# Routing of tokens in pieces inside the output stage of a mixer-and-experts layer, with a shorter hand-over to the experts

## Chip, cores, metric

One core of a Trainium2 chip runs the whole layer as one program. The metric is the device time of one execution in microseconds (us). TensorE (PE), VectorE (DVE), ScalarE (ACT), GpSimd (POOL) and the DMA issuer SyncE (SP) each run their own instruction stream and meet at semaphores.

## The reference, cut to what matters

2048 prompt tokens and 64 sample tokens (8 sequences of 8) go through one layer. The mixers leave `[y_pool, y_lru]`; after them come

```
mix = concat([y_pool, y_lru]) @ w_out
x1  = LN(ALPHA * x + (1 + g1) * mix) * ln1_g + ln1_b
u2  = x1 * (1 + sc2) + sh2
group logits = u2 @ w_group + b_group (4), expert logits = u2 @ w_route + b_route (4 x 4)
group = argmax; the top 2 experts inside it; weights = softmax(top 2) * softmax(group)[group]
y   = sum over the token's 2 experts of weight * (silu(u2 @ w_gate) * (u2 @ w_up)) @ w_down
out = LN(ALPHA * x1 + (1 + g2) * y) * ln2_g + ln2_b
```

All of it is fp32 (D = 1024, 16 experts of width 256).

## The kernel before

The 2112 tokens are 17 tiles of 128 (`NT`; the last has 64 rows). The program has four stages: the conditioning, input projection and mixers (to about 497 us in the trace); the **output stage** (to 735 us); the **routing** (to 791 us); the **experts** and the last layer norm (to the end). Each engine's instructions are in an order written out by hand, and each wait is a semaphore written by hand. fp32 products on PE are made of three matmuls of split operands (hi and lo parts), lines L1583 to L1585.

**Output stage, tile t.** PE: `out_proj` makes 48 matmuls of 512 columns in two halves of 24; inside the second half, after 9 of them (`k == 3`), stand the eight transposes of tile t-2 (`turn_u2`, L1534), and behind it the router of tile t-2 (`router`, L1736, 20 columns, waits for the evacuated transposes and for `rt_ok`). DVE: `ln_in(t)` (L1202 from PSUM, L1206, statistics L1212 to L1220), `ln_out(t-1)` (L1228, L1229: u2 of the tile, on which `turn_u2` waits), `router_out(t-2)` (L1233, signals `rt_ok`). ACT splits operands, takes the root, normalises (L831) and evacuates transposes. POOL makes, in turns, the lo part of a left operand (`y_lo(t+2)`, L587) and x1 of a tile in two whole-tile instructions (`x1_tile(t)`, L602 and L603); `ln_out(t)` waits for these two. SP stores x1 and u2 of each tile and loads the next operands.

**Routing**, all on DVE and for all 17 tiles at once: choices of group and experts (L1276 to L1296, each step waits for the one before), `m_ready`; PE counts, for 272 columns (tile, expert), the tokens ahead within a tile and in the tile (L1768, L1769); a running sum over the 17 tiles (L1307, 17 steps), the slots of each expert (L1310 to L1315), each token's row (L1318 to L1331), then three large one-hot tables (`hot_b`, L1340 to L1342; `hot_a`, L1345) from which 34 bf16 matmuls (L1774) make the token list `tok_i` (L1364). A **slot** is 128 rows of one expert; there are 48. POOL gathers the tokens of a slot with an indirect DMA (L637). Meanwhile expert 0's weights (SP, L446, issued after `rt_ok` 17) are split by ACT (L875) and POOL (`first_lo`, L623, six parts). Then DVE makes the routing weights (L1367 to L1378) and three weight tables (L1381, L1383), and PE another 34 matmuls (L1826) ahead of the first expert matmul. Each slot is then `gate_up`, `turn_x` of the next slot, `turn_h` and `down` on PE, with evacuations (L893, L1422) on ACT and DVE.

```
            with pe.Fori(2, NT // 2) as j:
                for b in range(2):
                    out_proj(2 * j + b, b, turn_before=lambda: turn_u2(2 * j + b - 2, b))
                    router(2 * j + b - 2)
```

Of the kernel before, what the change touches and what calls it, by code (L numbers as in the profile page):

```python
# [5 lines left out]
P = 128  # L6
D = 1024
KD = D // P
SEQ, DEC_B, DEC_T = 2048, 8, 8
# [20 lines left out]
OUT_EARLY = 6  # L30
ARENA = 21168
# [5 lines left out]
NZ = 6  # L37
# [47 lines left out]
def build(nc, A):  # L85
    with ExitStack() as ctx:
# [37 lines left out]
        def part_at(off, *shape):  # L124
# [53 lines left out]
        w_raw = [at(n * WE, WE) for n in (1, 0)]  # L178
# [10 lines left out]
        ln2_g, ln2_b, g2_s = at(6144, D), at(7168, D), at(8192, D)  # L189
        zt = [at(n * 1024, D) for n in (*range(6), *range(9, 20))]  # L190
        y_pair = [place(ada_arena, n * 1024, D) for n in range(2)]

        rt = [at(n * 272, NT, NE) for n in range(6)]
        rt_f = [at(1632 + n * 68, NT, NGR) for n in range(9)]
        r17 = [at(2248 + n * NT, NT) for n in range(10)]
        big_t = at(2424, NE, NT)
        lt_prod = at(2700, NE, NE)
        slot_ge = at(2960, SLOTS, NE)

        hot_b = at(14336, 3 * NT * SLOTS).bitcast(BF16).rearrange("p (k t v s) -> p k t v s", k=2, t=NT, v=3)  # L200
        hot_a = at(16784, 2 * NT * P // 2).bitcast(BF16).rearrange("p (k t r) -> p k t r", k=2, t=NT)
        tile_no = at(4146, 2, NT)
        e48 = [at(4184 + n * SLOTS, SLOTS) for n in range(10)]
        e16 = [at(3960 + n * NE, NE) for n in range(5)]
# [38 lines left out]
        pos_i = sb("pos_i", [P, 2, NT], I32)  # L243
# [21 lines left out]
            u2T_ok rt_mm rt_ok m_ready cnt_mm w_exp w_expd hot_ready idx_mm idx_ready w_raw0 w_raw1 xg0 xg1 xgT_mm  # L265
# [3 lines left out]
        z_in = [sem(f"z_in{n}") for n in range(NZ)]  # L269
        pair_in = sem("pair_in")  # L270

        ada_in = [sem(f"ada_k{k}") for k in range(KD)]
# [25 lines left out]
        def raw_part(buf, n):  # L298

            return w_raw2[:, ds(buf * -1 + 1, 1), n * SPLIT:(n + 1) * SPLIT].rearrange("p a n -> p (a n)")  # L300
# [7 lines left out]
        def _(sp):  # L308

            sp.dma_start(z_d[NTOK:NTOK + P, :], xpt_d[0]).then_inc(S["dump_in"], 16)  # L310
            for k in range(KD):
                sp.dma_start(w_ada[k], ada_d[k][:, 0:2048]).then_inc(ada_in[k], 16)
# [192 lines left out]
            for t in range(NT - 1):  # L505
# [3 lines left out]
                if t >= NZ:  # L509
                    sp.wait_ge(z_in[t % NZ], 16 * (t // NZ))  # L510
# [1367 lines left out]
```

## Time and profile before

| | |
|---|---|
| three runs | 1355.7, 1356.63 (median), 1358.93 us |
| the profiled execution | 1357.65 us; its span in the trace 1355.8 us |
| mean granted TensorE clock | 0.915 |
| busy in the span | PE 1129.9 us (83%), DVE 912.4 (67%), ACT 538.3 (40%), POOL 528.5 (39%) |
| output stage, routing, experts, last norm | to 735, to 792, to 1263, to 1356 us |

The shares are means over stages with different limits. The routing is a stretch of 56 us in which PE stands nearly still and DVE is the busy engine; in the output stage and with the experts it is the reverse. How PE's clock is read: 1.00 is its higher level (2.4 GHz), 0.50 its lower one (1.2 GHz), values between are means over a stretch that holds both.

### The profile page before, as it was taken

What the parts mean: (1) busy time and instruction counts of PE and PEld (TensorE: products, weight loads), DVE (VectorE), ACT (ScalarE), POOL (GpSimd) and SP (SyncE); (2) the same over time, 40 slices, a digit from 0 to 9 for tenths busy, and PEclk for the clock granted to TensorE, in tenths of its full rate; (3) what the DMA queues carried; (4) which work ended last, traced back from release to release, by engine and by line L of the source; (5) the groups of instructions that cost most, each with busy time, mean ns of one, the idle gap of its engine ahead of it and who ended that gap; (6) DMA issues with size and microseconds to landing.
All of it is one profiled execution on the core that took longest, in us unless ns stands there. A gap on an engine that the chain in (4) does not pass through costs nothing.

```text
span 1355.8 us, 23133 instructions
## 1 busy us (share of the span) xinstructions
PE 1129.9 (83%) x6461; PEld 940.3 (69%) x6462; DVE 912.4 (67%) x1844; ACT 538.3 (40%) x917; POOL 528.5 (39%) x540
## 2 busy tenths in 40 slices
PE   4889999999998688999995169999999999999200
PEld 1278988898888567888884057777777777888200
DVE  2675988898889485555554966556676666534398
ACT  0345435543542631222221134446555554433232
POOL 1411202220220225656652434545655464543365
PEclk8779999999998788999996589999999999999755
DMA  9604113312321463443435077887988887654673
GB/s 339 249 1 163 56 67 124 124 39 85 124 77 55 131 218 123 152 144 139 170 116 170 17 253 209 231 226 220 251 257 246 223 223 210 132 116 92 171 287 116
DMA packets 106187, 215.04 MB, mean 159 GB/s; under 512 B 18091, under 2 KB 67759, under 8 KB 103187
## 3 DMA queue, kind: packets, MB, share of 16 engines
q1 hardware_dynamic: 85004, 163.14, 34.8%
q0 software_dynamic: 20736, 50.89, 16.8%
q10 hardware_dynamic: 415, 0.63, 0.1%
q8 instruction: 15, 0.25, 0.1%
q14 instruction: 17, 0.14, 0.0%
HBM read 153.93 MB, written 85.96 MB: 177 GB/s over the span
## 4 chain that ended last, share of the span: by engine, by line
PE 57%; DVE 20%; DMA 6%; issue 6%; ACT 4%; DVEq 2%; SPq 2%; POOL 1%; ACTq 1%; POOLq 0%
PE bank L1583 16%; PE bank L1585 15%; PE bank L1584 15%; PE bank L1534 5%; DMA ada_arena<-in_w_ada 2%; PE bank L1658 2%; DVE arena L1515 1%; PE bank L1604 1%; DVE st L1498 1%; DVE arena L1206 1%; DVE parts L1415 1%; PE bank L1736 1%; DMA arena<-in_w_up 1%; DVEq L1408 1%; ACT parts L888 1%
## 5 line engine op out<-in xcount | busy, mean ns | idle before, releaser
L1583 PE MATMUL bank<-parts 128*128 128x256 f32 (+2 forms) x1616 | 570.7, 353 | 38.7 <-DVE parts L1422 15.9
L1585 PE MATMUL bank<-parts 128*128 128x256 f32 (+2 forms) x1616 | 554.2, 343 | 0.0
L1584 PE MATMUL bank<-parts 128*128 128x256 f32 (+2 forms) x1616 | 553.7, 343 | 0.0
L1583 PEld LDWEIGHTS bank<-parts 128*128 128x128 f32 x1616 | 310.1, 192 | 86.8 <-issue 36.2
L1585 PEld LDWEIGHTS bank<-parts 128*128 128x128 f32 x1616 | 309.5, 192 | 35.1
L1584 PEld LDWEIGHTS bank<-parts 128*128 128x128 f32 x1616 | 310.4, 192 | 31.5
L570 POOL TENSOR_TENSOR arena<-arena 128x256 f32<-128x256 f32 (+1 forms) x36 | 25.9, 722 | 311.9 <-DVE h_last L1139 276.6
L1534 PE MATMUL bank<-ident,arena 128*128 128x128 f32 (+3 forms) x792 | 120.4, 285 | 32.5 <-DVE arena L1229 12.9
L1534 PEld LDWEIGHTS bank<-ident,arena 128*128 128x128 f32 (+3 forms) x792 | 95.8, 148 | 64.3 <-issue 20.5
L1415 DVE TENSOR_TENSOR parts<-arena,parts x90 | 104.8, 1220 | 18.9 <-ACT parts L888 18.9
L913 ACT ACTIVATE arena<-bank,w_now 128x512 f32<-128x512 f32 x96 | 66.1, 688 | 126.4 <-PE bank L1585 72.9
L1449 DVE SCALAR_TENSOR_TENSOR arena<-bank,w_now,arena 128x512 f32<-128x512 f32 x96 | 69.3, 749 | 48.2 <-PE bank L1585 48.2
L888 ACT ACTIVATE parts<-arena x90 | 88.7, 1056 | 5.9 <-DMA arena<-in_w_down 5.9
L650 POOL DMA_INDIRECT z_d<-arena,dst_now x48 | 80.8, 1684 | 19.0 <-issue 19.0
L729 ACT ACTIVATE arena<-bank,proj_b 128x256 f32<-128x256 f32 x64 | 30.4, 475 | 142.2 <-PE bank L1585 142.2
L602 POOL TENSOR_TENSOR arena<-arena 128x1024 f32<-128x1024 f32 (+1 forms) x17 | 56.6, 3327 | 55.7 <-ACT arena L831 55.7
L1202 DVE TENSOR_TENSOR arena<-bank,arena 128x512 f32<-128x512 f32 (+1 forms) x34 | 21.8, 683 | 83.3 <-PE bank L1585 83.3
L893 ACT ACTIVATE parts<-bank 128x512 fp32r<-128x512 f32 x96 | 52.2, 595 | 37.0 <-PE bank L1534 34.6
L1422 DVE TENSOR_TENSOR parts<-bank,parts 128x512 fp32r<-128x512 f32 x96 | 61.8, 685 | 7.5 <-ACT parts L893 7.5
L898 ACT ACTIVATE arena<-bank 128x256 f32<-128x256 f32 x48 | 18.4, 384 | 108.9 <-PE bank L1585 107.7
L644 POOL COPY dst_now<-dst_i 128x2 int32 (+1 forms) x48 | 8.7, 181 | 130.6 <-ACT arena L913 130.6
L652 POOL DMA_INDIRECT ysamp_d<-arena,dst_now x48 | 53.6, 1116 | 14.6 <-issue 14.6
(270 smaller groups left out, 1538.5 us busy)
## 6 DMA issues: line engine op xcount, KB each, us to landing
arena<-in_w_gate SPq DMA_DIRECT2D x16, 1024.0 KB, 5.6
arena<-in_w_up SPq DMA_DIRECT2D x16, 1024.0 KB, 9.7
arena<-in_w_down SPq DMA_DIRECT2D x16, 1024.0 KB, 13.0
arena<-in_w_ada SPq DMA_DIRECT2D x14, 1024.0 KB, 5.7
ada_arena<-in_w_ada SPq DMA_DIRECT2D x8, 1024.0 KB, 17.0
arena<-in_x_prompt SPq DMA_DIRECT2D x8, 1024.0 KB, 6.9
yT_d<-arena SPq DMA_DIRECT2D x16, 512.0 KB, 5.1
arena<-yT_d SPq DMA_DIRECT2D x16, 512.0 KB, 4.7
```

Source lines behind the costliest of these rows:

```text
L602: o.step(pool.tensor_tensor(x1[b][0:n, :], z[b][0:n, :], row_tiles[0:n, 1, :], ALU.mult))
L650: pool.indirect_dma_start(out=z_d, out_offset=bass.IndirectOffsetOnAxis(ap=dst_now[b][:, 0:1], axis=0), in_=y_sb[b], in_offset=None, compu ...
L652: pool.indirect_dma_start(out=ysamp_d, out_offset=bass.IndirectOffsetOnAxis(ap=dst_now[b][:, 1:2], axis=0), in_=y_raw[b], in_offset=None, ...
L888: act.activation(part(w_hi, e & 1, n), raw_part(e & 1, n), ACT.Copy).then_inc(S["w_hi"], 1)
L913: act.activation(y_raw[b][:, 512 * h:512 * h + 512], bank[5 + h][:, :], ACT.Copy, scale=w_now[b][:, 0:1]).then_inc(S["y_act"], 1)
L1415: dve.tensor_tensor(part(w_lo, e & 1, n), raw_part(e & 1, n), part(w_hi, e & 1, n).bitcast(F32), ALU.subtract).then_inc(S["w_lo"], 1)
L1422: dve.tensor_tensor(xT_lo[:, k, :], bank[h][:, :].rearrange("p (k n) -> p k n", n=P), xT_hi[:, k, :].bitcast(F32), ALU.subtract).then_inc( ...
L1449: dve.scalar_tensor_tensor(y_sb[b][:, cols], bank[5 + h][:, :], w_now[b][:, 0:1], g2_row[:, cols], ALU.mult, ALU.mult).then_inc(S["y_dve"], 1)
L1534: return pe.transpose(out, in_, ident[0:rows, 0:rows])
L1583: pe.matmul(out, x_hi, w_hi, start=start, stop=False)
L1584: pe.matmul(out, x_hi, w_lo, start=False, stop=False)
L1585: return pe.matmul(out, x_lo, w_hi, start=False, stop=stop)
```

## The change

- **Routing by groups of tiles.** `ROUTE = ((0, 4), (4, 8), (8, 12), (12, 17))`. For a group (lo, hi), DVE makes the choice of group behind `ln_out` of step t = hi + 2 (7 instructions), the choice of experts behind that of step hi + 3 (19), and the rows with their part of `hot_a` behind that of step hi + 5 (9). PE makes a group's ranks (two matmuls of 64 columns) in step hi + 5. So steps 6, 7, 9, 10, 11, 13, 14 and 15 carry a piece; the rows of tiles 8 to 11 and all of tiles 12 to 16 are done behind the stage. The running sum over tiles is part of the choices, and the 17-step sum and the 272-column count are gone.
- **PE of the stage.** `router(t-3)` stands between the two halves of `out_proj(t)` instead of `router(t-2)` behind it; the transposes stand after 18 matmuls of the second half (`k == 6`) instead of 9. DVE's `router_out` is ahead of `ln_in`.
- **The stage's end.** DVE makes `ln_out(15)` ahead of `ln_in(16)`, and makes x1 of the last tile itself (2 instructions, L1347 and L1348 of the new file) in place of POOL.
- **Weights of experts 0 and 1.** Expert 0's load waits for the last x1, expert 1's for the last router output (before: for the weights of all slots). `first_lo`: parts 0 and 1 on POOL ahead of the gathers, 4 and 5 behind the first two gathers, parts 2 and 3 on DVE. ACT makes the scaled one-hot piece (`hot_part`) that DVE made.
- **Token list.** The one-hots are made in two halves with PE starting on the first; `tok_i` is ahead of the list of the slots' experts; a first `idx_ready` releases the gathers, a second everyone else.
- **Routing weights.** The three tables and 34 matmuls stand behind `gate_up(0)`, `turn_x(1)` and `turn_h(0)`.
- Buffers are placed anew; the last stage's loads have 8 semaphores instead of 6.

The diff, cut (`-` before, `+` after):

```
-            router_out(1)
-            with dve.Fori(2, NT // 2) as j:
-                    ln_in(2 * j + b, b, P, prompt_rows, j + 1)
-                    ln_out(2 * j + b - 1, 1 - b, P, prompt_rows, j + b, False)
-                    router_out(2 * j + b - 2)
+            for t in range(3, NT - 1):
+                router_out(t - 3)
+                ln_in(t, t % 2, P, prompt_rows, t // 2 + 1)
+                ln_out(t - 1, 1 - t % 2, P, prompt_rows, (t - 1) // 2 + 1, False)
+                for lo, hi in ROUTE:
+                    if t == hi + 2: choose_group(lo, hi)
+                    if t == hi + 3: choose_experts(lo, hi)
+                    if t == hi + 5: place_rows(lo, hi)
...
-                        if turn_before is not None and h == 1 and k == 3:
+                        if turn_before is not None and h == 1 and k == 6:
...
+            def ranks(lo, hi):
+                pe.wait_ge(S["m_ready"], i + 1)
+                pe.matmul(out[:, 0:n * NE], tri[:], flat(m_all[:, lo:hi]), start=True, stop=False)
+                pe.matmul(out[:, 0:n * NE], ones[:], flat(cum_all[:, lo:hi]), start=False, stop=True).then_inc(S["rank_mm"], 1)
+            def route(t):
+                router(t - 3, first=t == 3)
+                for lo, hi in ROUTE:
+                    if t == hi + 5: ranks(lo, hi)
+            for t in range(3, NT - 1):
+                out_proj(t, t % 2, turn_before=lambda: turn_u2(t - 2, t % 2), between=lambda: route(t))
...
             turn_x(0, 0, 1, first=True)
+            gate_up(0, 0)
+            turn_x(1, 1, 1)
+            turn_h(0)
             pe.wait_ge(S["hotw_ready"], 1)
...
-            gate_up(0, 0)
-            turn_x(1, 1, 1)
-            turn_h(0)
```

What it does to the order of instructions, at three places. First DVE in the output stage, behind `ln_in` of a middle tile. Before (L1228, L1229 are `ln_out`; L1233 `router_out`; then the loop begins again):

```order
L1228 TENSOR_TENSOR arena<-arena 128x1024 [waits u2T_mm]
L68 REGISTER_ALU
L1229 TENSOR_TENSOR arena<-arena 128x1024 [waits dve_order]
L1233 ISA [waits rt_mm]
L1233 TENSOR_TENSOR logits<-bank,arena 128x20
L1252 REGISTER_ALU
L1252 COMPARE_AND_BRANCH
```

In the change, step 7 (L1246 is the end of `ln_out`; L1263 to L1297 `choose_experts` of tiles 0 to 3; L1250 `router_out` and L1219 the next tile's `ln_in`):

```order
L1246 TENSOR_TENSOR arena<-arena 128x1024 [waits dve_order]
L1263 TENSOR_REDUCE ada_arena<-ada_arena 128x4
L1264 TENSOR_TENSOR ada_arena<-ada_arena 128x16 [waits dve_order]
L1265 TENSOR_TENSOR ada_arena<-ada_arena,prio 128x16 [waits dve_order]
...
L1292 TENSOR_TENSOR ada_arena<-ada_arena 128x64
L1294 TENSOR_TENSOR ada_arena<-ada_arena 128x64 [waits dve_order]
L1296 TENSOR_TENSOR ada_arena<-ada_arena 128x16 [waits dve_order] x4
L1297 MEMSET spare 1x1 [waits dve_order]
L1250 TENSOR_TENSOR logits<-bank,arena 128x20 [waits rt_mm]
L1219 TENSOR_TENSOR arena<-bank,arena 128x512 [waits mix_ready]
```

Nineteen instructions and a signal, nearly all of them waiting for DVE's own last result (`dve_order`), now stand between one tile's `ln_out` and the next tile's `router_out` and `ln_in`, where before the loop went straight on.

Second, DVE at the end of the stage, from the last tile's statistics on. Before (the two pairs L1228 and L1229 are `ln_out` of tiles 15 and 16; L1276 the first choice):

```order
L1228 TENSOR_TENSOR arena<-arena 128x1024 [waits u2T_mm,u2_st1,x1_ready]
L1229 TENSOR_TENSOR arena<-arena 128x1024 [waits dve_order]
L1233 TENSOR_TENSOR logits<-bank,arena 128x20 [waits rt_mm]
L1228 TENSOR_TENSOR arena<-arena 64x1024 [waits u2T_mm,u2_st0,x1_ready]
L1229 TENSOR_TENSOR arena<-arena 64x1024 [waits dve_order]
L1233 TENSOR_TENSOR logits<-bank,arena 128x20 [waits rt_mm]
L1233 TENSOR_TENSOR logits<-bank,arena 64x20 [waits rt_mm]
L1276 TENSOR_REDUCE arena<-logits 128x17 [waits consts,rt_ok]
```

In the change (L1245 and L1246 are `ln_out`, L1219 begins `ln_in(16)`, L1250 is a router output, L1305 begins the rows of tiles 8 to 11):

```order
L1245 TENSOR_TENSOR arena<-arena 128x1024
L1246 TENSOR_TENSOR arena<-arena 128x1024
L1219 TENSOR_TENSOR arena<-bank,arena 64x512 x2
...
L1250 TENSOR_TENSOR logits<-bank,arena 128x20
L1347 TENSOR_TENSOR arena<-arena 64x1024
L1348 TENSOR_TENSOR arena<-arena 64x1024
L1245 TENSOR_TENSOR arena<-arena 64x1024
L1246 TENSOR_TENSOR arena<-arena 64x1024
L1250 TENSOR_TENSOR logits<-bank,arena 128x20
L1305 TENSOR_TENSOR ada_arena<-ada_arena,bank 128x2x64
...
L1250 TENSOR_TENSOR logits<-bank,arena 64x20
L1263 TENSOR_REDUCE ada_arena<-logits 128x5
```

`ln_out(15)` (the first L1245, L1246) has moved ahead of the last tile's `ln_in` (L1219), the last x1 (L1347, L1348) has come in from POOL, and the rows of tiles 8 to 11 (from L1305) stand ahead of the last router output and the last choices (from L1263).

Third, PE behind the last router. Before (L1768 and L1769 are the counts, L1774 the token list's matmuls, L1534 the transposes of slot 0, L1826 the weight matmuls):

```order
L1768 MATMUL bank<-arena,tri 128x272 [waits m_ready]
L1769 MATMUL bank<-arena,ones 128x272
L1774 MATMUL bank<-arena 128x144 [waits hot_ready]
L1774 MATMUL bank<-arena 128x144 x16
...
L1534 MATMUL bank<-ident,arena 128x128 [waits xg0,idx_ready]
L1534 MATMUL bank<-ident,arena 128x128 x7
L1826 MATMUL bank<-arena 128x144 [waits hotw_ready]
L1826 MATMUL bank<-arena 128x144 x33
```

In the change (L1831 to L1833 are the counts and ranks of the last group, L1858 the token list, L1602 the transposes, L1651 the first expert matmul's wait):

```order
L1831 MATMUL bank<-ada_arena,ones 128x16 [waits m_ready]
L1832 MATMUL bank<-ada_arena,tri 128x80
L1833 MATMUL bank<-ada_arena,ones 128x80
L1858 MATMUL bank<-arena,ada_arena 128x144 [waits hot_part,hot_ready]
L1858 MATMUL bank<-arena,ada_arena 128x144 x16
...
L1602 MATMUL bank<-ident,arena 128x128 [waits xg0,idx_ready]
L1602 MATMUL bank<-ident,arena 128x128 x7
...
L1651 REGISTER_ALU [waits w_lo]
...
L1651 MATMUL bank<-parts 128x512
```

The 272-column counts have shrunk to 16 and 80 columns, and the 34 weight matmuls are gone from between the transposes and the first expert matmuls; they stand behind the 24 matmuls of `gate_up(0)` and ten transposes.

## Rows read from the trace of the kernel before

**Rows 1.** By stretch: length, busy PE, PEld, DVE, ACT, POOL; PEclk, DMA, GB/s.
```profile
717.44:735.60 18.16, 10.17 (x63) 9.25 (x62) 9.58 (x17) 4.69 (x7) 5.64 (x2) 0.65 0.28 87
735.60:742.70 7.10, 0.00 (x0) 0.00 (x0) 6.34 (x24) 0.00 (x0) 0.00 (x0) 0.50 0.84 270
742.70:767.50 24.80, 2.18 (x4) 1.17 (x4) 21.41 (x44) 6.16 (x8) 14.17 (x6) 0.50 0.18 71
767.50:780.50 13.00, 3.77 (x34) 3.30 (x34) 12.61 (x18) 0.00 (x0) 0.00 (x0) 0.62 0.00 1
780.50:791.70 11.20, 5.21 (x41) 4.84 (x42) 10.26 (x26) 2.48 (x3) 6.17 (x9) 0.54 0.40 121
791.70:813.20 21.50, 16.86 (x84) 13.32 (x81) 9.91 (x20) 9.36 (x14) 5.28 (x6) 1.00 0.95 330
```

**Rows 2.** PE timeline, first transposes of the stage and matmuls after (start, duration, idle before).
```profile
516.05 1.97 PE L1534 MATMUL bank<-ident,arena 128*128 128x128 f32 x8 [3.54 <-DVE arena L1229]
...
519.10 0.63 PE L1583 MATMUL bank<-parts 128*128 128x512 f32 x1
519.52 0.63 PE L1584 MATMUL bank<-parts 128*128 128x512 f32 x1
...
522.45 0.39 PE L1584 MATMUL bank<-parts 128*128 128x512 f32 x1
522.68 0.40 PE L1585 MATMUL bank<-parts 128*128 128x512 f32 x1
```

**Rows 3.** Waits of PE in 515 to 720 us (total, times, longest).
```profile
PE bank L1534 <- DVE arena L1229: 6.3, 6, 3.5
```

**Rows 4.** PE timeline, a router inside the stage.
```profile
689.91 1.86 PE L1736 MATMUL bank<-arena 128*128 128x20 f32 x16
```

**Rows 5.** DVE timeline, one tile of the stage.
```profile
634.24 1.29 DVE L1202 TENSOR_TENSOR arena<-bank,arena 128x512 f32<-128x512 f32 x2 [6.04 <-PE bank L1585]
635.67 3.33 DVE L1206 SCALAR_TENSOR_TENSOR arena<-arena 128x1024 f32<-128x1024 f32 x1
...
642.72 1.22 DVE L1229 TENSOR_TENSOR arena<-arena 128x1024 f32<-128x1024 f32 x1
```

**Rows 6.** POOL timeline, the two x1 instructions of that tile.
```profile
642.83 3.35 POOL L602 TENSOR_TENSOR arena<-arena 128x1024 f32<-128x1024 f32 x1 [4.91 <-ACT arena L831]
646.26 2.40 POOL L603 TENSOR_TENSOR arena<-arena 128x1024 f32<-128x1024 f32 x1
```

**Rows 7.** DVE timeline, end of the stage: `ln_out` of tiles 15 and 16.
```profile
722.26 1.23 DVE L1228 TENSOR_TENSOR arena<-arena 128x1024 f32<-128x1024 f32 x1
...
729.41 1.22 DVE L1228 TENSOR_TENSOR arena<-arena 64x1024 f32<-64x1024 f32 x1 [4.58 <-POOL arena L603]
```

**Rows 8.** DVE timeline, routing: small steps, slots, one-hot tables.
```profile
751.18 1.77 DVE L1312 TENSOR_SCALAR arena<-arena 128x16 f32<-128x16 f32 x1
752.98 9.46 DVE L1313 TENSOR_TENSOR arena<-lt,arena 128x256 f32<-128x256 f32 x1
...
762.93 0.17 DVE L1315 TENSOR_TENSOR arena<-arena 128x16 f32<-128x16 f32 x1
763.14 0.17 DVE L1317 TENSOR_SCALAR arena<-arena 128x16 f32<-128x16 f32 x1
...
767.49 1.86 DVE L1340 TENSOR_TENSOR arena<-iota_s,pos_f 128x1632 bf16<-128x1632 f32 x1
...
769.94 1.85 DVE L1342 TENSOR_TENSOR arena<-arena 128x1632 bf16<-128x1632 bf16 x1
771.83 4.76 DVE L1345 TENSOR_TENSOR arena<-iota_r,pos_f 128x2176 bf16<-128x2176 f32 x2
```

**Rows 9.** POOL timeline, the lo parts of expert 0.
```profile
747.98 14.17 POOL L623 TENSOR_TENSOR parts<-arena,parts 128x1024 fp32r<-128x1024 f32 x6 [18.60 <-ACT parts L875]
```

**Rows 10.** PE timeline, token list and routing weights.
```profile
774.31 3.89 PE L1774 MATMUL bank<-arena 128*128 128x144 bf16 x34 [29.42 <-DVE arena L1345]
...
788.43 3.51 PE L1826 MATMUL bank<-arena 128*128 128x144 bf16 x34 [0.62 <-DVE arena L1383]
```

More of the change, by code:

```diff
@@ L30 @@
 OUT_EARLY = 6
+ROUTE = ((0, 4), (4, 8), (8, 12), (12, 17))
+FIRST_DVE = (2, 4)
+FIRST_HI = 3
 ARENA = 21168
@@ L624, in _ @@
                                    ALU.subtract).then_inc(S["w0_lo"], 1)
+            for n in range(FIRST_DVE[0]):
+                first_lo(n)
             pool.wait_ge(S["idx_ready"], 1)
@@ L656, in _ @@
             gather(1, 1)
+            for n in range(FIRST_DVE[1], E_PARTS):
+                first_lo(n)
             for n in range(2, 6):
@@ new lines, in choose_experts @@
+            def choose_experts(lo, hi):
+                n = hi - lo
+                hot_g, hot_1, hot_2, esel = (f[:, 0:n] for f in f_b[0:4])
+                over_e = hot_g.unsqueeze(3).to_broadcast([P, n, NGR, EPG])
+                first_max(esel, n, m1[:, lo:hi], hot_1)
+                o.step(dve.scalar_tensor_tensor(esel, hot_1, -BIG, esel, ALU.mult, ALU.add))
+                first_max(esel, n, m2[:, lo:hi], hot_2)
+                if hi == NT:
+                    o.step(dve.tensor_tensor(hot_g, hot_g, bc(valid[:, lo:hi], NGR), ALU.mult))
+                for k, hot in enumerate((hot_1, hot_2)):
+                    o.did(dve.tensor_tensor(g4(e12[:, k, lo:hi]), over_e, hot.unsqueeze(2).to_broadcast([P, n, NGR, EPG]), ALU.mult))
+                o.wait()
+                o.step(dve.tensor_tensor(m_all[:, lo:hi], e12[:, 0, lo:hi], e12[:, 1, lo:hi], ALU.add))
+                for t in range(lo, hi):
+                    o.step(dve.tensor_tensor(cum_all[:, t + 1], cum_all[:, t], m_all[:, t], ALU.add))
+                dve.memset(spare[0:1, 0:1], 0.0).then_inc(S["m_ready"], 1)
@@ L1247, in _ @@
             dve.wait_ge(S["rt_in"], 64)
-            router_out(0)
-            ln_in(3, 1, P, prompt_rows, 2)
-            ln_out(2, 0, P, prompt_rows, 2, False)
-            router_out(1)
-            with dve.Fori(2, NT // 2) as j:
-                o.enter(j, 2, LN_STEPS)
-                for b in range(2):
-                    ln_in(2 * j + b, b, P, prompt_rows, j + 1)
-                    ln_out(2 * j + b - 1, 1 - b, P, prompt_rows, j + b, False)
-                    router_out(2 * j + b - 2)
@@ L1258, in _ @@
-            o.leave(NT // 2 - 2)
+            for t in range(3, NT - 1):
[3 more added lines that the diff above has]
+                for lo, hi in ROUTE:
+                    if t == hi + 2:
+                        choose_group(lo, hi)
+                    if t == hi + 3:
+                        choose_experts(lo, hi)
+                    if t == hi + 5:
+                        place_rows(lo, hi)
@@ L1299, in _ @@
[L1299 to L1303 removed]
+            choose_group(*ROUTE[-1])
+            choose_experts(*ROUTE[-1])
             n_e, slots_n, start_e, end_e = e16[0], e16[1], e16[2], e16[3]
[L1305 to L1307 removed]
@@ L1385, in slot_rows, with hot_weights @@
+            def hot_weights():
+                by_piece = lambda v: by_tok(wgt_b[:, v, :].rearrange("p (k t) -> p k t", k=2), SLOTS)
+                for v in range(2):
+                    o.did(dve.tensor_tensor(hot_b[:, :, :, v, :], one_hot, by_piece(v), ALU.mult))
+                o.wait()
+                dve.tensor_tensor(one_hot, one_hot, by_piece(2), ALU.mult).then_inc(S["hotw_ready"], 1)
             def slot_rows():
```

316 lines of the change are left out of this document (174 added, 142 removed).

## The prediction

> **What bounds the kernel now.** I read the engine shares first, then a table by stretch, then PE's waits, then the timelines of DVE and POOL side by side. The table is to show one thing: from the stage's last out-projection matmul (717.2 us) to the first expert matmul (791.7) PE is busy 21.4 of 74.5 us, and in the 24.8 us that hold the running sum, slots and rows it is busy 2.2 while DVE is busy 21.4 [rows 1]. There DVE's chain of small steps is the bound. In the output stage it is PE: a tile takes about 13.7 us, and DVE stands 6.0 us idle before each `ln_in` [rows 5]. The change carries part of the chain into these 6 us, so what matters is how long a step takes there.
>
 A small step costs 0.21 us from start to start when alone (762.93 to 763.14) [rows 8].
>
> **The change, stretch by stretch** (against the profiled execution, 1357.65 us, which stands 1.02 us over the median of the three runs).
>
> *1. Stage up to the last out-projection: +2.0.* The first transposes waited 3.54 us [rows 2] of PE's 6.3 us of such waits [rows 3]. Standing nine matmuls later hides 9 x 0.23 = 2.0 of it; the wait left is 1.5, too short to expect the drop that followed here: after 3.5 us of idling, matmuls at 519 us came every 0.42 us at half clock, against 0.23 at full clock at 522 us [rows 2]. The transposes themselves (1.97, half of it) and some seven matmuls by 0.19 make 2.3. So -4.3 (ends: -2.0, if the clock drops all the same; -4.7 if the wait goes too). The five other waits, 6.3 - 3.5 = 2.7, go: each is under 0.9 and 2.0 us are given: -2.7. Ranks are new work on PE: two matmuls of 544 columns took 2.2 us at half clock [rows 1]; a group's 128 columns take 0.3 by columns and 0.5 with a fixed cost like the router's 16 instructions in 1.86 us [rows 4]: +1.0 for the two groups inside.
>
> Then the pieces. `choose_experts` is 19 steps, 4.0 us alone; but it begins as `ln_out` ends, and that is when POOL's x1 pair begins (642.72 + 1.22 against 642.83) [rows 5, 6]. If its first step is held until both are over, 4.8 us, it needs 8.8 in a gap of 5.8: **3.0 us late** for the next tile. `place_rows` (9 steps, 2.7) is 1.7 late, `choose_group` (7 steps, 1.5) 0.5. Steps 6 and 7 then end 3.5 late, steps 9 to 11 and 13 to 15 5.2; steps 8 and 12 have no piece and win 5.8 back. PE feels it where it waits for u2: the transposes, just in time before, now stand 9 matmuls (2.0) and one router (1.7) later, slack 3.7. Behind these DVE steps are queued `mix_used` and `router_out`, so the next out-projection is late in turn. With the x1 pair alone PE waits only 5.2 - 3.7 = 1.5. If `y_lo`, 2.4 more, falls on a run of pieces as one fell on L1206 [rows 5], the three runs of steps cost 2.2, 3.9 and 0.9 (the last before its final lateness arrives), 7.0 together. L1313 waited for four POOL instructions [rows 8, 9], more than the three I count, so I take +8.0. Ends: 0 (steps slip in between two POOL instructions) and 14 (four in every run).
>
> *2. To the last choice (25.4 us, 717.2 to 742.6): +3.2.* Now `ln_in(16)` starts 5.2 late, and behind `ln_out(15)` (two of 1.23) [rows 7]: 7.7 instead of 0.3, +7.4. In return the 4.58 us idle for POOL before the last `ln_out` [rows 7] and what lies ahead of it: POOL's pair took 5.6 [rows 1], DVE makes both in 2.5, -3.1. The last choices are 26 steps with narrower tiles, 5.9 us against 7.0 [rows 1]: -1.1. Ends for the lateness: 0.6 and 7.6 in place of 5.2.
>
> *3. To the one-hots (24.8 us) [rows 1]: -12.1.* What remains: counts on PE 0.7, slots 2.2, rows of five tiles 3.0, first slots 2.0; 7.9 us. Two POOL parts of 2.36 [rows 9] fall among these, because expert 0's load now starts earlier and lands here: +4.8. 12.7 in place of 24.8. Ends for POOL's share: 0 and 4.8 more, if the steps wait for it twice.
>
> *4. To the token list (13.0) [rows 1]: -5.6.* The large `hot_a` pair, 4.76, is gone from here, the part scaled by the row is ACT's. Four halves of 0.93 (half of 1.86 and 1.85) [rows 8] are 3.7; PE starts after two of them and needs 2 x 1.95 [rows 10], ending at 5.8; DVE meanwhile makes two small steps and the 48 x 16 comparison, to 6.1; copying and three steps 1.3: 7.4. ACT's part, 0.9 by an estimate from its weight parts (5.8 us for six of 1024 columns [rows 1] counts 0.97 each), hides behind DVE's own half.
>
> *5. To the first expert matmul (11.2) [rows 1]: +1.5.* The 34 weight matmuls, 3.51 with the pitch to the next [rows 10], are gone. But DVE now has between `tok_i` and the evacuation of slot 0 six steps (1.3), the weights (2.2), two weight parts (2.5) and, if POOL's parts 4 and 5 get in first, 4.8 of waiting; with the evacuation 1.3 and hand-overs 0.6 that is 12.7. If they don't, 8.6: ends -2.6 and +1.7. I take the upper case because of L1313.
>
> *6. To slot 2 (21.5, of which PE is busy 16.9) [rows 1]: +1.1.* `gate_up(0)` now starts after a long idle, at half clock: nine pitches 0.19 longer [rows 2], +1.7. The weight matmuls, 2.5 by an estimate at full clock from their 3.51, come in, but fill 3.1 of the 4.6 us of waits. Ends -3 and +4.
>
> *7. Nothing:* expert 1's load hides behind the routing; loops written out give no wait (an instruction fetch, if late, would show as a wait at every new tile); the last norm is untouched. DMA queues on SP change places only: `store_tile(16)` now goes behind the load of expert 0, and the one-hots wait for that store, but all of stretch 3 lies between.
>
> Sum: 2.0 + 3.2 - 12.1 - 5.6 + 1.5 + 1.1 = **-9.9**: 1347.75 profiled, **1346.7** by the median.
>
> **A rule weighed against the trace.** The row first: L1313 was held over four POOL instructions [rows 8, 9]. The Trainium skill, page "SBUF — State Buffer", section "Who interferes with whom", says that the shared port pair is an exclusive lock for one whole instruction, which goes to whoever issues first. By it a step that stands ready should wait for one POOL instruction, at most 2.4 us, and the sum would be that of rival A; the trace speaks against it where POOL's instructions follow each other without a gap.
>
> **Rivals.**
> *A. A step gets in after one POOL instruction* (2.4 a piece instead of 4.8). `choose_experts` is then 0.6 late, the others not at all: the 8.0 go, stretch 2 gains 5.2 - 0.6 = 4.6, stretch 3 2.4. -9.9 - 15.0 = -24.9: 1331.7 by the median. For it: L1312 waited for less than one part [rows 8]; between L602 and L603 lies a gap of 0.08 us [rows 6]. Against it: L1313.
> *B. Slower: DVE never catches up.* A piece that waits makes `ln_in` late, so `y_lo` too falls upon the next piece. With three POOL instructions (7.2) for each piece the lateness is 2.9, 5.4 and 4.1 for the three kinds; three, three and two of them, less 2 x 5.8 won back, are 21.5 by the end of the stage against the 13.2 (8.0 + 5.2) counted above: -1.6 left, 1355.0 (no change). With four, as L1313 [rows 8], it is 39.9: +16.8. It decides from 3.2 instructions a piece; halfway, at 3.5, it gives +7.6: 1364.2. Against it: POOL itself is idle 4.9 us before L602 [rows 6], and x1 waits for a late DVE too.
> *C. The gain behind the stage is eaten by POOL's parts* (upper ends of 3 and 5, two more clock drops of 2.3 in 1): -9.9 + 4.8 + 0.2 + 4.6 = -0.3: 1356.3.
>
> **How the numbers follow.** Forecast 0.58 (1340 to 1352.5 by its own ends), A 0.17, three instructions or C 0.15, B 0.10. About 0.3% (4.1 us) is what a measurement of this kernel can tell from no change: faster (under 1352.6) is the forecast with few exceptions and A, 0.73; same 0.17; slower 0.10. The range reaches down to A (1331) and up to the no-change cases (1359), and leaves B out.
>
> **What would show it.** Right: DVE's first two-operand step of a piece lasting up to 4.8 us under L602 and L603; PE waits for `ln_out` of 1 to 4 us in the tiles behind steps 7 and 11; the last `ln_in` some 7 us behind its matmul; `m_ready` to one-hots 12 to 13 us; no PE wait over 2 us at the first transposes. Wrong: pieces of 4 us with no long step (A), a tile period that stays over 16 us through the stage (B), POOL's parts falling after the one-hots, or a first expert matmul at full clock.

## The result and the profile after

The changed kernel takes **1336.76 us** (median of four runs) against 1356.16 for the kernel before beside it: a ratio of 0.9857, 95% interval 0.984 to 0.9874, some 19.4 us. The prediction was 1346.7. The sign was right, but the forecast gain is half of what came. The time lies in the range that was given (1331 to 1359), but below the forecast's own ends (1340 to 1352.5): the range held it only because it reached down to rival A. The kernel before came to 1356.2 to 1356.8 in every session; one execution of a later run (all pieces behind the stage) took 3980.63 us and is left out of its time.

The profiled executions (spans of 1355.8 and 1335.3 us) divide at the same places of the program:

| stretch | before | after | difference | predicted |
|---|---|---|---|---|
| 1 start to the end of the last out-projection | 717.2 | 711.85 | -5.3 | +2.0 |
| 2 to the end of the last choices | 25.4 | 29.3 | +3.9 | +3.2 |
| 3 to the one-hots | 24.8 | 9.2 | -15.6 | -12.1 |
| 4 to the token list | 13.0 | 7.5 | -5.5 | -5.6 |
| 5 to the first expert matmul | 11.2 | 14.5 | +3.3 | +1.5 |
| 6 to slot 2 | 21.5 | 22.7 | +1.2 | +1.1 |
| 7 to the end | 542.6 | 540.2 | -2.4 | 0 |

Two profiles of one kernel differ too: a second one of the change had its last out-projection end at 716.1 us and 564.7 us from the first expert matmul to the end, where this one has 562.9 and the kernel before 564.1. So stretch 7 shows no effect, and stretch 1 is known to some 4 us; what rests on less is taken from several runs below.

By stretch, the changed kernel's table (same columns as in [rows 1]; the first window holds stretch 2 up to the last router, the second the rest of it, then 3 to 6):

```profile
711.85:732.85 21.00, 11.93 (x69) 10.97 (x68) 17.47 (x44) 3.17 (x6) 0.55 (x1) 0.62 0.39 132
732.85:741.16 8.31, 0.00 (x0) 0.00 (x0) 7.36 (x29) 2.95 (x3) 2.58 (x2) 0.50 1.06 380
741.16:750.34 9.18, 1.57 (x6) 1.35 (x6) 7.97 (x21) 0.00 (x0) 2.20 (x1) 0.50 0.75 271
750.34:757.86 7.52, 4.24 (x34) 3.94 (x34) 6.99 (x13) 5.46 (x8) 0.00 (x0) 0.50 0.00 0
757.86:772.40 14.54, 1.95 (x9) 1.58 (x9) 11.86 (x22) 3.46 (x5) 10.64 (x11) 0.50 0.35 109
772.40:795.06 22.66, 21.48 (x114) 17.36 (x115) 16.44 (x32) 9.36 (x14) 4.65 (x6) 0.87 0.49 164
```

PE's 8.3 us of standing still for the last choices (7.1 before) are followed by 9.2 us where 24.8 were [rows 1], with 8.0 of them DVE's own work. In the last line the clock is 0.87, against 1.00 before: part of the first gate product ran at half clock.

PE's waits in the output stage and at its end (515 to 735 us), against one line of 6.3 us before, up to 720 us [rows 3]:

```profile
PE bank L1807 <- ACT arena L832: 5.0, 1, 5.0
PE bank L1807 <- DVE logits L1250: 4.0, 2, 3.5
PE bank L1602 <- DVE arena L1246: 3.1, 2, 2.5
```

Up to the end of the last out-projection only 2.5 (first transposes), 0.5 and 0.6 us of these fall; the 3.5 and the 5.0 come behind it. The first transposes, and the last router output, with which the stage ends for DVE:

```profile
515.05 1.71 PE L1602 MATMUL bank<-ident,arena 128*128 128x128 f32 x8 [2.53 <-DVE arena L1246]
```

```profile
732.85 0.17 DVE L1250 TENSOR_TENSOR logits<-bank,arena 64x20 f32<-64x20 f32 x1 [0.58 <-PE bank L1807]
```

DVE in step 7, where the choice of experts for tiles 0 to 3 stands (start, duration):

```profile
593.27 1.23 DVE L1246 TENSOR_TENSOR arena<-arena 128x1024 f32<-128x1024 f32 x1
594.41 0.16 DVE L1263 TENSOR_REDUCE ada_arena<-ada_arena 128x4 f32<-128x16 f32 x1
594.61 2.18 DVE L1264 TENSOR_TENSOR ada_arena<-ada_arena 128x16 f32<-128x16 f32 x1
596.82 0.17 DVE L1265 TENSOR_TENSOR ada_arena<-ada_arena,prio 128x16 f32<-128x16 f32 x1
...
597.23 2.04 DVE L1267 TENSOR_TENSOR ada_arena<-ada_arena 128x16 f32<-128x16 f32 x1
```

and POOL beside it, the two x1 instructions:

```profile
593.42 3.34 POOL L607 TENSOR_TENSOR arena<-arena 128x1024 f32<-128x1024 f32 x1 [1.45 <-ACT arena L840]
596.83 2.41 POOL L608 TENSOR_TENSOR arena<-arena 128x1024 f32<-128x1024 f32 x1
```

The piece holds two long steps, not one: L1264 ends with the first x1 instruction (596.79), L1267 with the second (599.27). In between two steps run at 0.17. The piece takes 7.5 us instead of the 8.8 of the sum. The same pattern stands in all eight pieces: 5.3 us for a choice of group, 6.4 for rows, 7.5 for a choice of experts, but for one of 9.7, in step 11, in which a third instruction of POOL, a `y_lo`, fell (DVE, then POOL):

```profile
658.23 2.93 DVE L1296 TENSOR_TENSOR ada_arena<-ada_arena 128x16 f32<-128x16 f32 x4
```

```profile
658.70 2.42 POOL L592 TENSOR_TENSOR parts<-arena,parts 128x1024 fp32r<-128x1024 f32 x1 [2.44 <-ACT parts L822]
```

The last statistics, and the steps that POOL's parts of expert 0 held:

```profile
717.72 1.27 DVE L1219 TENSOR_TENSOR arena<-bank,arena 64x512 f32<-64x512 f32 x2
...
737.96 3.08 DVE L1296 TENSOR_TENSOR ada_arena<-ada_arena 128x16 f32<-128x16 f32 x5
...
742.06 1.60 DVE L1359 TENSOR_TENSOR ada_arena<-ada_arena,iota 128x272 f32<-128x272 f32 x1
```

```profile
738.58 4.78 POOL L628 TENSOR_TENSOR parts<-arena,parts 128x1024 fp32r<-128x1024 f32 x2 [26.18 <-ACT parts L879]
```

The last `ln_in` starts 5.9 us behind its matmul (711.85). The two parts straddle the end of the last choices (741.16): five steps of L1296 took 3.08 where in the versions without these parts they took 1.01, and L1359 1.60 instead of 0.44.

Last, the hand-over to the experts, DVE, POOL and PE:

```profile
757.65 0.21 DVE L1398 SCALAR_TENSOR_TENSOR tok_i<-ada_arena 128x48 int32<-128x48 f32 x1
...
760.84 5.26 DVE L1426 CAST wgt_b<-wgt_rest 128x34 bf16<-128x34 f32 x1
766.13 2.36 DVE L1411 TENSOR_TENSOR parts<-arena,parts 128x1024 fp32r<-128x1024 f32 x2
...
770.77 1.29 DVE L1479 TENSOR_TENSOR parts<-bank,parts 128x512 fp32r<-128x512 f32 x2 [2.11 <-issue]
```

```profile
760.36 1.00 POOL L644 DMA_INDIRECT arena<-u_d,tok_now  x1 [0.16 <-issue]
761.39 4.66 POOL L628 TENSOR_TENSOR parts<-arena,parts 128x1024 fp32r<-128x1024 f32 x2
```

```profile
763.21 1.94 PE L1602 MATMUL bank<-ident,arena 128*128 128x128 f32 x8 [6.47 <-DMA arena<-u_d,tok_now]
772.40 0.79 PE L1651 MATMUL bank<-parts 128*128 x1 [7.24 <-DVE parts L1479]
772.98 0.63 PE L1652 MATMUL bank<-parts 128*128 x1
773.41 0.63 PE L1653 MATMUL bank<-parts 128*128 x1
```

A conversion of 34 columns (L1426) lasts 5.26 us, from within the gather to the end of POOL's parts 4 and 5 (the same step takes 0.18 where none of them runs beside it); two weight parts follow, then 2.1 us in which DVE shows no work, then the evacuation of slot 0 (L1479), and PE starts 7.24 us after its transposes, at a pitch of 0.43 us.

### The profile page after: what moved, and what is told of

It reads as the page before. It is cut to its first block and busy times, and to the rows that moved or that the text cites. A ratio compares the mean times of both kernels' runs of the same rounds, so it can differ in the third digit from the quotient of the medians.

```text
span 1335.3 us, 23072 instructions
## 1 busy us (share of the span) xinstructions
PE 1129.0 (85%) x6475; PEld 939.9 (70%) x6476; DVE 955.4 (72%) x1941; ACT 538.9 (40%) x919; POOL 518.6 (39%) x536
## 5 line engine op out<-in xcount | busy, mean ns | idle before, releaser
L1651 PE MATMUL bank<-parts 128*128 128x256 f32 (+2 forms) x1616 | 569.7, 353 | 42.0 <-DVE parts L1479 19.1
L1651 PEld LDWEIGHTS bank<-parts 128*128 128x128 f32 x1616 | 309.2, 191 | 91.4 <-issue 40.6
L1602 PE MATMUL bank<-ident,arena 128*128 128x128 f32 (+3 forms) x792 | 119.8, 284 | 19.1 <-DMA arena<-u_d,tok_now 6.5
L1602 PEld LDWEIGHTS bank<-ident,arena 128*128 128x128 f32 (+3 forms) x792 | 95.8, 148 | 49.6 <-issue 9.9
L607 POOL TENSOR_TENSOR arena<-arena 128x1024 f32<-128x1024 f32 x16 | 52.4, 3277 | 45.9 <-ACT arena L840 45.9
L1479 DVE TENSOR_TENSOR parts<-bank,parts 128x512 fp32r<-128x512 f32 x96 | 61.7, 684 | 9.5 <-ACT parts L910 7.4
L1090 DVE RECIPROCAL arena<-arena 128x256 f32<-128x256 f32 (+1 forms) x36 | 58.3, 1620 | 1.2
L644 POOL DMA_INDIRECT arena<-u_d,tok_now x48 | 53.1, 1106 | 9.1 <-issue 9.1
```

Of the source, the lines that this page charges most:

```text
L644: pool.indirect_dma_start(out=xg[b], out_offset=None, in_=u2_d, in_offset=bass.IndirectOffsetOnAxis(ap=tok_now[b][:, 0:1], axis=0)).then_i ...
L1090: o.step(dve.reciprocal(q_t[:, 0:n], q_t[:, 0:n]))
L1479: dve.tensor_tensor(xT_lo[:, k, :], bank[h][:, :].rearrange("p (k n) -> p k n", n=P), xT_hi[:, k, :].bitcast(F32), ALU.subtract).then_inc( ...
L1602: return pe.transpose(out, in_, ident[0:rows, 0:rows])
L1651: pe.matmul(out, x_hi, w_hi, start=start, stop=False)
```

## Experiments

The times are medians; the change itself came to 1336.76 and, in a second session, 1337.11. Differences are against the mean of the two, 1336.9, and a difference of two such runs is known to some 3 us.

**All pieces behind the stage.**

```
-                for lo, hi in ROUTE:
-                    if t == hi + 2:
-                        choose_group(lo, hi)
...
+            for n, (lo, hi) in enumerate(ROUTE):
+                choose_group(lo, hi)
+                choose_experts(lo, hi)
+                if n:
+                    place_rows(*ROUTE[n - 1])
...
-                    if t == hi + 5:
-                        ranks(lo, hi)
...
+            for lo, hi in ROUTE:
+                ranks(lo, hi)
```

The added lines stand behind the last router output (DVE) and the last router (PE).

> All pieces of the routing are made behind the output stage, everything else as in the change. Theory 1 (the pieces are nearly free inside the stage: the trace of the change shows only 1.1 us of PE waits behind them, and 3.4 us of lateness at the last statistics): 21.9 us of steps come back behind the stage (three groups by 1.5 + 4.0 + 2.7 us, less the 2.7 that stood there already) and about 4 us of waits go: +17 to +18 us, about 1354. Theory 2 (the price of the prediction: 8.0 us of PE waits and 5.2 of lateness): 21.9 - 13.2 = +8.7, about 1345.5.

Measured 1357.25 us, against the kernel before 1.0003 (0.9989 to 1.0017). So no gain of all that the change does besides the pieces can be measured, and the pieces are worth 20.3 us. Theory 2 is out; theory 1 was 2 to 3 us short, because more steps come back than its 21.9 us. The trace (PE, then DVE, then PE):

```profile
512.80 1.97 PE L1597 MATMUL bank<-ident,arena 128*128 128x128 f32 x8 [4.11 <-DVE arena L1246]
```

```profile
723.84 0.17 DVE L1250 TENSOR_TENSOR logits<-bank,arena 64x20 f32<-64x20 f32 x1 [3.48 <-PE bank L1802]
```

```profile
787.91 0.79 PE L1646 MATMUL bank<-parts 128*128 x1 [7.65 <-DVE parts L1474]
```

From the last router output to the first expert matmul it takes 64.1 us, against 39.6 in the change (732.85 to 772.40): 24.5 us come back. The rows of tiles 8 to 11, which the 21.9 leave out, fill a wait for the last router in the change; here DVE idles 3.48 us there. So the pieces cost 24.5 - 20.3, some 4 us, in the stage by the times. By the traces, from the first transposes to the last router output, it is 211.0 us here and 217.8 in the change: 6.8 us, of which 1.6 fall before the end of the last out-projection (195.2 against 196.8) and 5.2 behind it. Over the nine profiles whose stage is as in the change, the 217.8 is anything from 215.7 to 219.6, so the two agree: a price of 4 to 7 us.

**The transposes back at the ninth matmul.**

```
-                        if turn_before is not None and h == 1 and k == 6:
+                        if turn_before is not None and h == 1 and k == 3:
```

> The transposes of each tile go back 9 matmuls (2.0 us) earlier in PE's order. Theory 1 (the slack of 3.7 us, 2.0 of it from this move, is what swallows the lateness of the pieces): the first wait grows by 2.0, the small waits of the other tiles (2.7 us in the kernel before) return, and the tile behind steps 9 to 11 (5.2 us late) waits 2 more: +6 to +8 us, about 1344, and waits for the u2 of DVE in many tiles. Theory 2 (pieces hardly ever make u2 late, the move itself is of no worth): only the first wait grows, +2 us, about 1339.

Measured 1340.16: +3.2, between the theories. PE's waits for u2 in that profile are 4.6 us at the first transposes and 2.9 in 4 other places, against 2.5 and 0.6 in the change: the first wait grew and small waits came back, as theory 1 has it, but they are short, the longest 1.5 us.

**POOL's x1 made longer, and shorter.** In `x1_tile` the line of the multiplication stands twice, or that of the addition is left out (then the bias of the layer norm is missing, and only the time is of use):

```
                 o.step(pool.tensor_tensor(x1[b][0:n, :], z[b][0:n, :], row_tiles[0:n, 1, :], ALU.mult))
+                o.step(pool.tensor_tensor(x1[b][0:n, :], z[b][0:n, :], row_tiles[0:n, 1, :], ALU.mult))     (twice)
-                pool.tensor_tensor(x1[b][0:n, :], x1[b][0:n, :], row_tiles[0:n, 2, :], ALU.add)             (once)
```

> POOL makes the first of the two x1 instructions of every tile twice (same result), so that 7.2 us instead of 4.8 lie on each piece. Theory 1 (each two-operand step that stands ready waits for one POOL instruction, so a piece is held once more, 2.0 us; the 3.7 us of slack on PE were nearly used up): the pieces grow by 2.0 us each, the run of steps 9 to 11 ends about 11 us late instead of 5.2, PE waits 5 to 8 us more in the stage and the last statistics start later: +6 to +10 us, about 1345. Theory 2 (the pieces find their time in the gaps of POOL anyway and PE does not feel them): +2 us or less.

Measured 1354.98, +18.0: above even theory 1's upper end. PE's waits in the stage and at its end:

```profile
PE bank L1808 <- DVE logits L1251: 11.6, 4, 6.7
PE bank L1603 <- DVE arena L1247: 6.0, 3, 5.0
```

and DVE, then POOL, in step 7 there (lines stand one lower in that kernel):

```profile
596.80 2.16 DVE L1265 TENSOR_TENSOR ada_arena<-ada_arena 128x16 f32<-128x16 f32 x1
...
599.40 2.04 DVE L1268 TENSOR_TENSOR ada_arena<-ada_arena 128x16 f32<-128x16 f32 x1
...
601.89 2.08 DVE L1265 TENSOR_TENSOR ada_arena<-ada_arena 128x16 f32<-128x16 f32 x1
604.00 2.37 DVE L1266 TENSOR_TENSOR ada_arena<-ada_arena,prio 128x16 f32<-128x16 f32 x1
```

```profile
601.50 2.44 POOL L609 TENSOR_TENSOR arena<-arena 128x1024 f32<-128x1024 f32 x1
603.89 2.45 POOL L592 TENSOR_TENSOR parts<-arena,parts 128x1024 fp32r<-128x1024 f32 x1
```

Four steps of that piece are held, one for each POOL instruction (a `y_lo` among them), and it takes 11.6 us. Of the waits, 5.0 us stand at the first transposes, ahead of any piece, and 6.7 behind the last out-projection; behind the pieces within the stage they are 5.9 us, against 1.1 in the change, and 4.9 of them are the router's wait for DVE's output (`logits`). So PE does feel the longer pieces; how the 18.0 us divide was not worked out further.

> POOL makes only the first of the two x1 instructions of tiles 0 to 15: the bias of the first layer norm is left out there (so the routing falls a little differently; the output stage and its end are what is compared). 2.4 us instead of 4.8 lie on each piece. Theory 1 (doubling one of them showed the stage at the edge of its slack; the change still pays some 1 us of PE waits and 3.4 us of lateness at the last statistics for the second instruction): the pieces shrink by 2.0 us each, the waits on PE in the stage but for the first go, the last statistics start 2 to 4 us sooner: -3 to -6 us against the change, 1331 to 1334. Theory 2 (what is left of lateness there comes from the number of steps, not from POOL): -1 us or less.

Measured 1329.24, -7.7: more than theory 1 said. Up to the last out-projection no wait of PE is left, the first transposes included, the last `ln_in` starts 2.1 us behind its matmul, and from the first transposes to the last router output it takes 210.9 us, as without the pieces.

**Where the parts of expert 0 land, and the last x1.**

```
-            sp.wait_ge(S["x1_ready"], NT)
-            load_expert(0, 0, static=True)
             store_tile(NT - 1, 0, NS)
             sp.wait_ge(S["rt_ok"], NT)
+            load_expert(0, 0, static=True)
```

> Expert 0's load waits for the last router output again, as in the kernel before, some 6 us later. Theory 1 (in the change POOL's first two parts fell partly ahead of the last choice's end and held only two steps there, 3.4 us in all; where they land matters little, since two held steps cost about the same anywhere): within 2 us of the change, 1336.8. Theory 2 (the early landing is what saved the 3.5 us by which the stretch from the last choice to the one-hots beat the prediction): +3 us or more, about 1340.

Measured 1338.08: +1.1, theory 1. The other one, x1 of the last tile back on POOL:

```
             x1_tile(NT - 2, 1, NT // 2 - 1)
+            x1_tile(NT - 1, 0, NT // 2, NS)
-            o.step(dve.tensor_tensor(x1[0][0:NS, :], z[0][0:NS, :], row_tiles[0:NS, 1, :], ALU.mult))
...
```

> x1 of the last tile goes back from DVE to POOL, nothing else. Theory 1 (the sum of the prediction: 5.6 us on POOL against 2.5 on DVE, on the path): +3 us, about 1340. Theory 2 (the last x1 waits for ACT's norm in any case and DVE has no idle time left there, so two DVE instructions less pay for the slower pair): within 1 us.

Measured 1340.01: +3.1, as theory 1 and the sum had it, though the time alone does not rule theory 2 out; in the trace the last router output comes 22.9 us behind the last out-projection instead of 21.0.

**The weight matmuls back ahead of the first gate product.**

```
-            gate_up(0, 0); turn_x(1, 1, 1); turn_h(0)
             pe.wait_ge(S["hotw_ready"], 1)
...
+            gate_up(0, 0); turn_x(1, 1, 1); turn_h(0)
```

> The 34 weight matmuls go back ahead of the first gate product. Theory 1 (the sum of the prediction: their move takes 3.5 us off the way to the first expert matmul and gives 1.1 back later, but in the change DVE makes the three tables, 5.5 us, only behind the evacuation of slot 0, so they end 5 us after the first expert matmul now starts): +5 to +7 us, about 1342.5. Theory 2 (the first gate product then runs at full clock and the weight matmuls are gone from behind it, which pays for most of it): +2 us or less.

Measured 1345.92: +9.0, beyond theory 1. PE waits for the third table (L1434), and from the second expert matmul on it runs at full clock (783.18 to 783.40):

```profile
778.73 4.26 PE L1910 MATMUL bank<-arena,ada_arena 128*128 128x144 bf16 x34 [12.50 <-DVE arena L1434]
782.74 0.60 PE L1651 MATMUL bank<-parts 128*128 x1
783.18 0.39 PE L1652 MATMUL bank<-parts 128*128 x1
783.40 0.39 PE L1653 MATMUL bank<-parts 128*128 x1
```

**The hand-over.** First the register loads alone, then the routing weights too go behind the evacuation of slot 0; at last four lo parts of expert 0 on DVE (`FIRST_DVE = (0, 4)`).

```
-            weights()
...
+            x_evac(0)
             slots = [next_expert(s) for s in range(3)]
-            x_evac(0)
+            weights()
             hot_weights()
```

> DVE's three register loads of the slots' experts go behind the evacuation of slot 0. Theory 1 (the 2.1 us without work ahead of the evacuation are these loads, and the evacuation is what the first expert matmul waits for): -2.1 us, about 1334.7. Theory 2 (those 2.1 us are something else, for example a wait for ACT's evacuation): no change, 1336.8.

Measured 1335.35: -1.6, too little to tell the theories apart by the time; but in its profile the evacuation follows the weight parts at once, and the first expert matmul comes 12.5 us behind the token list instead of 14.5: theory 1.

> DVE's routing weights (ten small steps, one of them held 5.3 us by POOL's two parts) and the register loads go behind the evacuation of slot 0. Theory 1 (DVE's chain sets the first expert matmul): it starts 5 to 6 us earlier, right behind ACT's evacuation; the weight tables end later but before the first gate product is needed: -5 to -6 us, about 1331. Theory 2 (what DVE is late with there is wanted just as soon behind it): the start moves, but the weight matmuls or the hidden product then wait, and no more than 2 us are left: about 1335.

Measured 1332.59: -4.4; the first expert matmul comes 9.0 us behind the token list instead of 14.5, and 1.3 us of the gain return as a wait for the hidden product. Nearer theory 1.

> As with the routing weights behind the evacuation of slot 0, and the first two lo parts of expert 0 made by DVE too (it waits 3.8 us for ACT there), so that POOL holds no step of the last choices and of the slots. Theory 1 (POOL's parts cost DVE 3.4 us on the path there, and two parts of 1.2 fit into the wait for ACT): -3 us against that run, about 1329.5. Theory 2 (the two parts on DVE are late for the first expert matmul, or POOL's parts 4 and 5 then hold them): no gain, about 1332.6.

Measured 1330.55, -6.4 against the change; the -2.0 against that run alone is within the noise. It ran again beside the change:

> The change itself, unaltered, on the same chip as the next run, as its yardstick: 1336.8 us again, within 2 us.

> The version with the routing weights behind the evacuation of slot 0 and four of expert 0's lo parts on DVE, again, beside the change on one chip. If its gain is real: 6 to 7 us under the change. If it was the difference of two chips or hours: 3 us or less.

Measured 1337.11 and **1329.30 us**: -7.8, and 0.9806 of the kernel before (0.9784 to 0.9828). The hand-over there, DVE and PE:

```profile
754.52 4.62 DVE L1411 TENSOR_TENSOR parts<-arena,parts 128x1024 fp32r<-128x1024 f32 x4
...
760.86 1.48 DVE L1479 TENSOR_TENSOR parts<-bank,parts 128x512 fp32r<-128x512 f32 x2 [1.54 <-ACT parts L910]
```

```profile
759.03 1.94 PE L1601 MATMUL bank<-ident,arena 128*128 128x128 f32 x8 [6.64 <-DMA arena<-u_d,tok_now]
762.67 0.79 PE L1650 MATMUL bank<-parts 128*128 x1 [1.70 <-DVE parts L1479]
```

DVE's four parts fill most of the wait for ACT (1.54 us are left), and PE waits 1.70 us instead of 7.24.

**What lets a held step in.** In the kernel before, POOL waits for each of the six parts to end before it begins the next:

```
                                    ALU.subtract).then_inc(S["w0_lo"], 1)
+                pool.wait_ge(S["w0_lo"], n + 1)
```

> The kernel before, with one thing added: POOL waits for the end of each of expert 0's six lo parts before it begins the next (its two x1 instructions have such a wait between them, these parts had none). Theory 1 (a held DVE step gets in at a boundary where POOL itself has to wait, and not where its next instruction already stands ready): the step of 256 columns that was held over four parts, 9.46 us, is held over one, up to 2.5 us; more steps are held once each; the stretch from the last choice to the one-hots shrinks by 3 to 7 us, the whole to about 1351. Theory 2 (it was the kind of step that was held, whatever POOL does in between): the same step takes 9 us again, no change.

Measured 1355.26, 0.9986 of the kernel before (0.9972 to 1.0). DVE's steps of the slots there, one line lower than in [rows 8], and POOL's parts:

```profile
750.86 1.76 DVE L1313 TENSOR_SCALAR arena<-arena 128x16 f32<-128x16 f32 x1
752.66 0.42 DVE L1314 TENSOR_TENSOR arena<-lt,arena 128x256 f32<-128x256 f32 x1
...
753.57 1.79 DVE L1316 TENSOR_TENSOR arena<-arena 128x16 f32<-128x16 f32 x1
...
755.61 2.46 DVE L1319 TENSOR_TENSOR arena<-arena 128x272 f32<-128x272 f32 x1
```

```profile
747.68 15.36 POOL L623 TENSOR_TENSOR parts<-arena,parts 128x1024 fp32r<-128x1024 f32 x6 [18.33 <-ACT parts L876]
```

L1314, which had been held 9.46 us as L1313 [rows 8], took 0.42. Instead L1316, L1319 and others are held once each, and the slots are done 7.7 us sooner (755.36 against 763.10), but the one-hots come only 2.1 us sooner, since the parts then lie on the rows. Theory 1 for that step, and no gain that can be measured.

And behind parts 4 and 5 of the change:

```
                 first_lo(n)
+                pool.wait_ge(S["w0_lo"], n + 1 - FIRST_DVE[1] + FIRST_DVE[0])
```

> The change, with such a wait of POOL behind each of expert 0's lo parts 4 and 5. Theory 1: the conversion of 34 columns that was held 5.26 us is held up to 2.5, and the next two-operand step after it, the first weight part on DVE, once: the first expert matmul comes 0 to 2.5 us sooner, 1334 to 1337. Theory 2: 5.3 us again, no change.

Measured 1338.21. DVE:

```profile
762.82 2.96 DVE L1427 CAST wgt_b<-wgt_rest 128x34 bf16<-128x34 f32 x1
765.81 4.58 DVE L1412 TENSOR_TENSOR parts<-arena,parts 128x1024 fp32r<-128x1024 f32 x2
```

The conversion is held 2.96 instead of 5.26, but the two weight parts behind it take 4.58 instead of 2.36. The first expert matmul comes 0.1 us sooner after the token list: theory 1's lower end.

## Why the prediction was right and wrong

**The step that failed** is the price of the pieces in stretch 1, "so I take +8.0". With the pieces in the stage and without them, the stretch from the first transposes to the end of the last out-projection is 196.8 and 195.2 us: 1.6. In the nine profiles with this stage (the two of the change, and seven runs that alter only what follows) it is 198.2 on the mean, so 3.0, and 5.2 at most. The lateness of 5.2 in stretch 2 was about right: from the last out-projection's end to the last router output it is 21.0 us with the pieces and 15.8 without them, 5.2 in this profile, 4.2 on the mean. Together they are 4 to 7 us, by times and traces, where the sum had 13.2. My terms for all other edits come to -9.9 + 21.9 - 13.2 = -1.2, or +1.4 with the 24.5 us that came back; the run with the pieces behind the stage stands 0.4 us over the kernel before by its ratio (-1.5 to +2.3), and agrees with both.

Three things made 8.0 out of little. *The hold.* I let the first step of a piece wait for both x1 instructions, 4.8 us at once. In fact it waits for one, other steps run, and a second waits for the second: 4.2 us, and the pieces are 1.0 to 1.3 us shorter than I had them, 3.4 over a run of three, where the slack is 3.7. *The third instruction.* I laid a `y_lo` on each of the three runs; it fell on one piece of eight. With the lengths measured, the lateness of steps 9 to 11 against the gap of 5.8 is 0.6 - 0.5 + 3.9 = 4.0 instead of 7.6 (an estimate), hardly over the slack; PE's waits behind step 11 are 1.1 us. *The row.* I went above my own case because L1313 had outlasted four instructions [rows 8, 9]. That row came from parts which POOL issues without a wait of its own; x1's second instruction waits for the first, and there the step gets in. The added wait let the same step through: 0.42 us in place of 9.46. It is not the whole rule, for L1312 in that row got in after one part without it. The Trainium skill, page "SBUF — State Buffer", section "Who interferes with whom", has the lock last for one whole instruction of whoever came first. In the pieces the trace agrees, step by step; where POOL's next instruction already stood ready, L1313 and L1426 were held over more than one, which that sentence does not cover.

**Rival A** named this mechanism and gave 1331.7, but it counted one hold of 2.4 a piece. There are two, so the truth lay between. **Rival B** did not happen, but it stood close: with one POOL instruction more the kernel takes 1354.98. That its three instructions a piece had been priced at 1355.0 is luck to this digit: it laid all of them on one step, and either figure is known to 2 us or so. **Rival C** did not happen: POOL's parts cost 3.2 us ahead of the one-hots, not 9.6.

**Stretch by stretch.** 1: the first wait shrank by 1.0 and not 2.0, and the half clock stayed (matmuls 0.43 us apart until 518.7 in this trace), which is the end that I gave as -2.0 in place of -4.3; the five small waits went as said; the pieces brought 1.1 us of waits. In the second profile of the change they brought 2.8. 2: +3.9 for +3.2; the last `ln_in` came 5.9 behind its matmul instead of 7.7 (1.1 without the pieces, so the 2.5 us that I gave to `ln_out(15)` were mostly hidden), and 2.1 us of POOL's parts fell here. 3: my 7.9 us of remaining steps were 8.0; of POOL's 4.8 only 1.2 fell here. The later load (+1.1 us) shows that their place is worth little. 4: 7.5 for 7.4. 5: 14.5 for 12.7; the hold of two parts was right, the 2.1 us of register loads were forgotten, and the 8.6 of the lower end does not follow from the terms shown (12.7 less 4.8 is 7.9). 6 was right. Of the single edits that could be priced alone, x1 on DVE (3.1) was right as far as its noise allows; the later weight matmuls were worth 9.0 once DVE's tables stood behind the evacuation, and the later transposes 3.2 where I had 7.0 (-4.3 and -2.7; 4.7 with the half clock).

**The signs named ahead.** The last `ln_in` some 7 us late (5.9) and the half clock at the first gate product came; a first step held up to 4.8, PE waits of 1 to 4 us behind steps 7 and 11 (none, and 0.5 and 0.6), 12 to 13 us from the last choice to the one-hots (9.2) and a wait under 2 us at the first transposes (2.5) did not. Of the signs of being wrong none came as written: the pieces held two long steps, not none.

**Open.** Which held step gets in between two POOL instructions that follow without a wait is not known. L1312 before and one of the five L1296 in the change (16 columns each) got in between two parts, L1313 (256 columns) and L1426 (34) did not; L1359 stood beside the last part and tells nothing. The added wait let both L1313 and L1426 in sooner, but x1 without its own wait was not tried. My "when both operands lie in SBUF" is too narrow too: L1312 and L1426 read one tensor and were held. The first transposes of the stage start anywhere from 512.4 to 516.1 us in these profiles, and no cause was looked for.

## What to carry to other kernels

A chain of small steps can be worth most of its length (here 20.3 of 24.5 us) if it is cut into pieces that nearly fit another stage's gaps; add up lateness run by run, against the place where the bound engine first waits, and test the edge by lengthening what stands beside it: here 2.4 us a tile more on POOL took the whole gain back. Price a hold between two engines from a row in which the other engine issues as it will in the new place, and not from the worst row in the trace. At a hand-over, order an engine's work by what the next engine waits for: moving ten small steps and three loads behind one evacuation, and filling its wait with the parts, gave 7.8 us more.

## What was not expected of the hardware

Register loads of three values held DVE for 2.1 us. DVE steps that POOL held got in where POOL waited for its own last result (in all eight pieces the first hold ended with the first x1 instruction, though the second began 0.1 us behind it; 0.42 us for the same step that took 9.46 without the wait). And the edge is sharp on both sides: one x1 instruction of POOL more a tile cost 18.0 us, one less gave 7.7, about as much as the pieces cost; what the shorter x1 saves outside the pieces was not separated.
